# A fused two-block transformer kernel on one Trainium2 core: the first chunk behind a norm multiplied without the norm's root, in three feed-forwards of block one

## The chip, the cores and the metric

One of the eight cores of a Trainium2 chip runs the whole program. Times are device microseconds (us), the median of several runs. A core has five engines that work side by side and wait for each other by semaphores: TensorE (PE, matmuls), VectorE (DVE), ScalarE (ACT), GpSimd (POOL) and SyncE (SP), which here only issues the loads of weights.

## The reference

Two blocks of two layers each on x of 256 tokens by 1024. Only block one's feed-forwards are touched. Each of its layers has two, `f1` ahead of the mixers and `f2` behind them:

```python
D_MODEL, SEQ, D_FF = 1024, 256, 2816
def _rms_norm(x, g):
    xf = x.astype(jnp.float32)
    y = xf * lax.rsqrt(jnp.mean(xf * xf, axis=-1, keepdims=True) + EPS)
    return (y * g.astype(jnp.float32)).astype(x.dtype)
def _modulate(xn, shift, scale):
    return xn * (1 + scale[:, None, :]) + shift[:, None, :]
def _swiglu(x, w_in, w_out):
    gate, up = jnp.split(x @ w_in, 2, axis=-1)
    return (jax.nn.silu(gate) * up) @ w_out
...
mod = cond @ ada_w[l] + ada_b[l]
sh1, sc1, g1, sh2, sc2, g2, sh3, sc3, g3 = jnp.split(mod, N_MOD, axis=-1)
hn = _modulate(_rms_norm(h, norm_g[l, 0]), sh1, sc1)
h = h + 0.5 * g1[:, None, :] * _swiglu(hn, ffn1_w_in[l], ffn1_w_out[l])
...
hn = _modulate(_rms_norm(h, norm_g[l, 2]), sh3, sc3)
h = h + 0.5 * g3[:, None, :] * _swiglu(hn, ffn2_w_in[l], ffn2_w_out[l])
```

In words: each token (a column in the kernel) is divided by its root mean square, scaled and shifted per feature, and multiplied by `w_in`. A token's root is a factor of its whole column, so it commutes with the product; the shift does not carry it.

## The kernel before

**Layout.** Activations `h` lie as 8 k-tiles of 128 features by 256 tokens. A product takes weights in chunks of 1024 by 256 (8 k-tiles, 1 MB). SP loads them one after the other into a ring of four slots.

**Three terms.** For precision every operand is split in two fp32r parts. ScalarE rounds half a chunk at a time to `w_hi` (`round_half`, L1264), GpSimd subtracts to get `w_lo` (L700), and the activations have `hn` (high) and `hn_lo`. `terms` (L734) does hi x hi, hi x lo and lo x hi: six matmuls of 256 columns for a k-tile of a chunk (two column halves c, three terms), 48 for a chunk. `w_hi` and `w_lo` have two slots.

**Feed-forward** (`ffn`). `w_in` has 22 chunks in 11 pairs p: chunk 2p is the gate, 2p + 1 the value. Chunk 2p goes to PSUM bank 0 or 2, chunk 2p + 1 to bank 1 or 3, both column halves in one bank. ScalarE takes the SiLU (L1352), VectorE multiplies (L1836), and the product is split in two parts `gated` (L1359 on ScalarE, L1839 on VectorE). Bank reuse makes chunk 2p + 4 wait for pair p. In `f1` of pairs 1 to 8 and in layer 0's `f2` of pairs 1 to 6, VectorE also sums an `ada` chunk of 2 MB (L1701 to L1719), which will be modulation values later; SP loads it in the same sequence, into two buffers at the start of the arena. Then come 16 chunks of `w_out` in four groups g; after each, VectorE adds two tiles of the residual to `h` (marks `h f1 0` to `h f1 7` and so on).

**A norm.** ScalarE squares each new tile (L1292), VectorE adds the squares of tiles 0 to 5 up, and TensorE (`norm_sum`, L860 and L863) multiplies that sum and the squares of tiles 6 and 7 with a matrix of ones. ScalarE forms the root as exp(-0.5 ln x) (L1298, L1300). Then the chain runs through `h` by tiles: VectorE multiplies by gain and root into one of two PSUM tiles `normed` (L1796), ScalarE adds the shift and rounds to `hn` (L1324), VectorE forms `hn_lo` (L1805). Chunk 0 of the product follows with a loop of its own (L765, L766, L769), which takes each k-tile as it comes:

```python
for k in range(n if first else 0):
    kx, kw = k_tiles(phase, i)[0] + k0 + k, half * 4 + k
    pe.wait_ge(scalar_done, eng.at(f"hi {first} {kx}"))
    for c in range(2):
        ws = cols(c)[0]
        mm(outs[c], w_hi[:, q, kw, ws], hn[:, kx], start=kx == 0 and c == 0, stop=False)
        mm(outs[c], w_lo[:, q, kw, ws], hn[:, kx], start=False, stop=False)
    pe.wait_ge(vector_done, eng.at(f"split {first} {kx}"))
```

Six chunk 0s in the program wait for a root in this way: `f1`, `z` (the mixers' input) and `f2` of both layers. In `f1` of layer 0 the root is there early, since x comes from outside. In block two the first chunk is multiplied without the root already: `weigh` (L1310, L1311) makes tiles that carry the gain alone, and the root is applied to results.

**Order.** Each engine's program is written out by hand, one function per engine, and runs in that order; a wait holds up everything behind it on its engine.

## Time and profile before

| | |
|---|---|
| median of 3 runs | 1916.34 us (1914.74 to 1918.4) |
| the profiled execution | 1915.01 us |
| its span, first to last instruction | 1913.2 us |
| mean granted TensorE clock | 0.989 |
| TensorE, busy | 1856.1 us, 97% |
| weight loads of TensorE, busy | 1799.4 us, 94% |
| GpSimd, ScalarE, VectorE, busy | 1437.8, 988.2 and 916.9 us |
| matmuls at L734 on the chain that ended last | 78% of the span |
| mean DMA rate | 208 GB/s |

The median and the span don't measure the same: the runs include what lies around the first and the last instruction. In a timeline each line is an instruction, or several equal ones merged (x2), with its start, its length, and in brackets how long the engine had been idle before it and who released it. Matmuls overlap: a 256-column one is shown with 0.28 us but follows its neighbour in 0.11 us at full clock, so starts are to be compared, not lengths. The granted clock is a share of 2.4 GHz.

### The profile page before, as it was taken

How to read it: one execution, taken by the hardware profiler on the slowest of the kernel's cores; microseconds unless marked ns; L12 is line 12 of the kernel's file. 1: busy time of each engine (PE TensorE's matmuls, PEld its weight loads, DVE VectorE, ACT ScalarE, POOL GpSimd, SP SyncE). 2: the span in 40 equal slices, each digit the busy share in tenths (PEclk: the TensorE clock that was granted, in tenths of full speed). 3: DMA queues.
4: the chain of work that ended last, by engine and by line, in shares of the span. 5: the costliest groups of instructions: out<-in, count | busy, mean ns of one | idle time of the engine just before them, and what ended most of it. 6: DMA issues, size and time to landing. Idle time of an engine off the chain costs nothing.

```text
span 1913.2 us, 37040 instructions
## 1 busy us (share of the span) xinstructions
PE 1856.1 (97%) x15544; PEld 1799.4 (94%) x15544; DVE 916.9 (48%) x1817; ACT 988.2 (52%) x1531; POOL 1437.8 (75%) x660
## 2 busy tenths in 40 slices
PE   6999998999999999889999999999999999999999
PEld 3999997899999998879999998999999998999999
DVE  3676497485148676854132634253311634343321
ACT  2544466544454455655545345576554345575543
POOL 1888772688878887548888965588897965587896
PEclk8999999999999999999999999999999999999999
DMA  9999762695589896436556643455665643355662
GB/s 318 344 359 333 235 192 72 219 362 192 183 296 367 298 312 191 135 123 227 195 169 198 213 144 121 133 180 178 195 208 163 214 145 124 129 188 174 192 208 88
DMA packets 357109, 397.94 MB, mean 208 GB/s; under 512 B 9048, under 2 KB 319056, under 8 KB 356944
## 3 DMA queue, kind: packets, MB, share of 16 engines
q1 hardware_dynamic: 356032, 395.04, 63.0%
q8 instruction: 122, 2.00, 0.4%
q10 hardware_dynamic: 912, 0.55, 0.1%
q14 instruction: 43, 0.35, 0.1%
HBM read 394.51 MB, written 1.05 MB: 207 GB/s over the span
## 4 chain that ended last, share of the span: by engine, by line
PE 88%; SPq 3%; DVE 3%; ACT 2%; DMA 1%; POOL 1%; issue 1%; ACTq 0%; DVEq 0%
PE bank L734 78%; PE bank L1011 1%; PE bank L969 1%; POOL w_lo L700 1%; PE bank L765 1%; PE bank L769 1%; PE bank L766 1%; SPq L594 1%; ACT arena L1402 1%; PE bank L725 1%; SPq L604 1%; DVE arena L1926 1%; SPq L536 1%; DMA ring<-in_ffn_w_in 1%; SPq L575 1%
## 5 line engine op out<-in xcount | busy, mean ns | idle before, releaser
L700 POOL TENSOR_TENSOR w_lo<-ring,w_hi 128x1024 fp32r<-128x1024 f32 (+2 forms) x656 | 1437.5, 2219 | 460.6 <-ACT w_hi L1264 459.6
L1264 ACT ACTIVATE w_hi<-ring 128x1024 fp32r<-128x1024 f32 (+2 forms) x656 | 629.1, 983 | 394.5 <-PE bank L734 382.8
L734 PE MATMUL bank<-hn,w_hi 128*128 128x256 f32 x2752 | 770.6, 280 | 8.5 <-ACT arena L1581 4.9
L734 PE MATMUL bank<-hn_lo,w_hi 128*128 128x256 f32 x2752 | 763.2, 277 | 0.0
L734 PE MATMUL bank<-hn,w_lo 128*128 128x256 f32 x2752 | 763.2, 277 | 0.0
L734 PEld LDWEIGHTS bank<-hn,w_hi 128*128 128x128 f32 x2752 | 517.9, 188 | 13.7 <-ACT arena L1581 6.5
L734 PEld LDWEIGHTS bank<-hn,w_lo 128*128 128x128 f32 x2752 | 518.1, 188 | 0.0
L734 PEld LDWEIGHTS bank<-hn_lo,w_hi 128*128 128x128 f32 x2752 | 516.7, 188 | 0.9 <-issue 0.5
L734 PE MATMUL bank<-gated,w_hi 128*128 128x256 f32 x1408 | 241.9, 277 | 0.0
L734 PEld LDWEIGHTS bank<-gated,w_hi 128*128 128x128 f32 x1408 | 212.8, 188 | 0.0
L734 PE MATMUL bank<-gated,w_lo 128*128 128x256 f32 x704 | 195.2, 277 | 0.0
L734 PE MATMUL bank<-up,w_hi 128*128 128x256 f32 x1024 | 174.2, 276 | 0.0
L1704 DVE SCALAR_TENSOR_TENSOR bank<-arena,cond,bank 128x512 f32<-128x512 f32 x204 | 154.2, 756 | 7.3
L734 PEld LDWEIGHTS bank<-up,w_hi 128*128 128x128 f32 x1024 | 154.0, 188 | 0.0
L734 PE MATMUL bank<-up,w_lo 128*128 128x256 f32 x512 | 141.3, 276 | 0.0
L734 PEld LDWEIGHTS bank<-gated,w_lo 128*128 128x128 f32 x704 | 132.1, 188 | 0.0
L1352 ACT ACTIVATE arena<-bank 128x512 f32<-128x512 f32 x44 | 26.3, 598 | 155.4 <-PE bank L734 155.0
L1836 DVE TENSOR_TENSOR bank<-arena,bank 128x512 f32<-128x512 f32 x44 | 30.6, 696 | 155.7 <-PE bank L734 155.7
L1402 ACT ACTIVATE arena<-arena,stat 128x128 f32<-128x128 f32 x120 | 53.2, 444 | 91.1 <-DVE stat L1893 43.9
L734 PEld LDWEIGHTS bank<-up,w_lo 128*128 128x128 f32 x512 | 96.1, 188 | 0.0
L734 PE MATMUL bank<-w_hi,hn 128*128 128x256 f32 x288 | 84.0, 292 | 0.0
L734 PE MATMUL bank<-w_hi,hn_lo 128*128 128x256 f32 x288 | 80.3, 279 | 0.0
(237 smaller groups left out, 2440.2 us busy)
## 6 DMA issues: line engine op xcount, KB each, us to landing
ring<-in_ffn_w_in SPq DMA_DIRECT2D x88, 1024.0 KB, 7.3
ring<-in_w_in SPq DMA_DIRECT2D x72, 1024.0 KB, 5.2
arena<-in_ada_w SPq DMA_DIRECT2D x35, 2048.0 KB, 10.9
ring<-in_w_up SPq DMA_DIRECT2D x32, 1024.0 KB, 5.5
ring<-in_w_down SPq DMA_DIRECT2D x32, 1024.0 KB, 5.1
ring<-in_ffn_w_out SPq DMA_DIRECT2D x32, 768.0 KB, 5.4
ring<-in_ffn_w_out SPq DMA_DIRECT2D x32, 640.0 KB, 4.1
ring<-in_w_in SPq DMA_DIRECT2D x16, 512.0 KB, 3.7
```

The costliest lines, as they stand in the source:

```text
L536: queue.dma_start(dst, src).then_inc(rows_in, 16)
L575: sp.dma_start(ada[:, c % 2], ada_source(layer, c)).then_inc(ada_in[c % 2], 16)
L594: sp.dma_start(ring[:, s, k:k + n, :], src).then_inc(weights_in[s], 16)
L604: sp.dma_start(dst, src).then_inc(params_in, 16)
L700: pool.tensor_tensor(w_lo[:, q, ks], ring[:, r, k0:k0 + n], w_hi[:, q, ks], ALU.subtract) \
L725: i = pe.transpose(dst, src, ident[0:n, 0:n])
L734: last = mm(out, a, b, start=start and i == 0, stop=stop and i == 2)
L1264: f(w_hi[:, q, half * 4:half * 4 + n], ring[:, r, k0:k0 + n], ACT.Copy).then_inc(weights_rounded, 1)
L1352: f(act_tmp[:, j], bank[:, 2 * j], ACT.Silu).then_inc(silu_done, eng.step(f"{s} silu {p}", silu_done))
L1402: f(t, t, ACT.Exp, bias=st[:, b + j:b + j + 1], scale=scale, accum_out=st[:, 10 + 2 * m + j:11 + 2 * m + j]) \
L1704: stt(part, src[:, k], col(cond, k), part, ALU.mult, ALU.add).then_inc(vector_done, eng.step())
L1836: tt(bank[:, 2 * j], act_tmp[:, j], bank[:, 2 * j + 1], ALU.mult) \
```

## The change

It concerns `f2` of layer 0, `f1` and `f2` of layer 1. Layer 0's `f1` (`whole`) and both `z` keep the old way.

- While the products ahead of the norm run, ScalarE scales each new tile of `h` by the gain alone, twice (`weigh_parts`): to `normed` in PSUM and, rounded, to a new tile set `weighted_hi`; VectorE subtracts to `hn_lo` (`weighed_parts`). Squares, sum and root stay.
- `weighted_hi` has 258 columns that are used: column 256 holds the shift and 257 its rounding rest (`shift_columns`). The product so yields the 256 token columns and two that sum to the shift's contribution.
- TensorE (`weighted_product`) multiplies chunk 0 with these tiles, its column halves in banks 0 and 7, and does the norm's sum between k-tiles 1 and 2.
- ScalarE makes the root, copies it for all tokens (`token rstd`) and then runs the old chain for `hn`, which chunk 1 now takes tile by tile. In between it rounds chunk 1's second half and both halves of chunk 2, where the old chain had only chunk 1's second half.
- VectorE (`apply_root`) sums the two shift columns and multiplies both halves by the root into bank 0. The SiLU of pair 0 is done in halves with the shift as bias, behind the rounding of chunk 3.
- `hn_lo` is shared: VectorE waits for chunk 0's halves before it overwrites tiles 0 and 4. `weighted_hi` lies where an `ada` buffer lies: SP waits for chunk 0's end ahead of one `ada` load per place.

The diff's core (line numbers of hunks are the file's):

```diff
@@ -466,6 +466,8 @@
...
+        weighted_hi = {n: rounded(f"weighted_{n}", start, KT, S + 8) for n, start in (("f1", 4096), ("f2", 7168))}
@@ -571,6 +573,8 @@
...
                     sp.wait_ge(ada_summed, n - 1)
+                if (layer, c) in ((1, ADA_FIRST + 1), (0, 17), (1, 17)):
+                    sp.wait_ge(weights_used, eng.at("used f2in 0" if c == 17 else "used f1in 0"))
@@ -741,6 +745,28 @@
...
+            def weighted_product(phase, n, outs):
+                pe.wait_ge(vector_done, eng.at(f"h {n} {4 if n == 'f2' else 6}"))
+                for half in range(2):
+                    half_ready(phase, 0, half)
+                    for k in range(4):
+                        kx = 4 * half + k
+                        if kx == 2:
+                            norm_sum(n)
+                        pe.wait_ge(scalar_done, eng.at(f"weighted hi {n} {kx}"))
+                        for c in range(2):
+                            ws = slice(c * P, (c + 1) * P)
+                            mm(outs[c], w_hi[:, 0, kx, ws], weighted_hi[n][:, kx, 0:S + 2], start=kx == 0, stop=False)
+                            mm(outs[c], w_lo[:, 0, kx, ws], weighted_hi[n][:, kx, 0:S + 2], start=False, stop=False)
+                        pe.wait_ge(vector_done, eng.at(f"weighted split {n} {kx}"))
+                        for c in range(2):
+                            last = mm(outs[c][:, 0:S], w_hi[:, 0, kx, c * P:(c + 1) * P], hn_lo[:, kx],
+                                      start=False, stop=kx == KT - 1)
+                    last.then_inc(weights_used, eng.step(f"used {phase} 0" if half else f"half used {phase} 0", weights_used))
@@ -929,11 +955,16 @@
...
+                whole = (s, layer) == ("f1", 0)
...
+                        if not whole and p == r == 0:
+                            weighted_product(s + "in", s, (bank[:, 0, 0:S + 2], bank[:, 7, 0:S + 2]))
+                            continue
...
-                        product(s + "in", (2 * p + r,), (b[:, 0], b[:, 1]), first=s if p == r == 0 else None,
+                        product(s + "in", (2 * p + r,), (b[:, 0], b[:, 1]),
+                                first=s if p == 0 and r == (0 if whole else 1) else None,
@@ -1310,6 +1338,19 @@
...
+            def weigh_parts(n, ks):
+                gains = der[:, 0:8] if n == "f1" else der[:, 16:24]
+                for k in ks:
+                    act.wait_ge(vector_done, eng.at(f"h {n} {k}"))
+                    if k >= 2:
+                        act.wait_ge(vector_done, eng.at(f"weighted split {n} {k - 2}"))
+                    gain = gains[:, k:k + 1]
+                    f(normed[:, k % 2], h[:, k], ACT.Identity, scale=gain).then_inc(scalar_done, eng.step())
+                    f(weighted_hi[n][:, k, 0:S], h[:, k], ACT.Identity, scale=gain) \
+                        .then_inc(scalar_done, eng.step(f"weighted hi {n} {k}"))
@@ -1329,6 +1370,32 @@
...
+            def weighted_and_norm(n, phase, shift):
+                take_squares(n, (6, 7))
+                weigh_parts(n, (6, 7))
+                norm_root(n)
+                f(rstd[:], rstd[:], ACT.Exp, scale=-0.5).then_inc(scalar_done, eng.step(f"token rstd {n}"))
+                for k in range(KT):
+                    act.wait_ge(vector_done, eng.at(f"normed k {n} {k}"))
+                    f(hn[:, k, :], normed[:, k % 2], ACT.Identity, bias=mod[:, shift + k:shift + k + 1]) \
+                        .then_inc(scalar_done, eng.step(f"hi {n} {k}"))
+                    if k == 1:
+                        round_half(phase, 1, 1)
+                    if k == 4:
+                        act.wait_ge(weights_in[slot_of(phase, 2)], eng.arrived(phase, 2))
+                        round_half(phase, 2, 0)
+                    if k == 6:
+                        round_half(phase, 2, 1)
@@ -1336,21 +1403,29 @@
...
-            def ffn(s, following):
+            def ffn(s, following, whole=False):
...
+                    if p == 0 and not whole:
+                        round_chunk(s + "in", 3)
+                        act.wait_ge(vector_done, eng.at(f"root applied {s}"))
+                        for c in range(2):
+                            f(act_tmp[:, 0, c * S:(c + 1) * S], bank[:, 0, c * S:(c + 1) * S], ACT.Silu,
+                              bias=small[:, 60 + c:61 + c]) \
+                                .then_inc(silu_done, eng.step(f"{s} silu 0" if c else None, silu_done))
+                    else:
+                        act.wait_ge(weights_used, eng.at(f"used {s}in {2 * p}"))
@@ -1544,14 +1622,16 @@
...
                 take_squares("f2", (0, 1))
+                weigh_parts("f2", (0, 1))
...
                 round_chunk("f2in", 0)
                 take_squares("f2", (4, 5))
+                weigh_parts("f2", (4, 5))
                 act.wait_ge(weights_in[slot_of("f2in", 1)], eng.arrived("f2in", 1))
                 round_half("f2in", 1, 0)
-                take_squares("f2", (6, 7))
-                norm("f2", "f2in", 48, late=((4, 1),))
+                weighted_and_norm("f2", "f2in", 48)
@@ -1799,6 +1879,8 @@
...
                         dve.wait_ge(scalar_done, eng.at(f"hi {n} {k - 1}"))
+                        if used and k in (1, 5):
+                            dve.wait_ge(weights_used, eng.at(f"{'half ' if k == 1 else ''}used {used} 0"))
@@ -1819,7 +1901,39 @@
...
+            def weighed_parts(n, g):
+                for k in (2 * g, 2 * g + 1):
+                    dve.wait_ge(scalar_done, eng.at(f"weighted hi {n} {k}"))
+                    tt(hn_lo[:, k, :], normed[:, k % 2], weighted_hi[n][:, k, 0:S], ALU.subtract) \
+                        .then_inc(vector_done, eng.step(f"weighted split {n} {k}"))
+            def shift_columns(n, at_):
+                shifts, wide = mod[:, at_:at_ + 8], weighted_hi[n]
+                dve.tensor_copy(wide[:, :, S], shifts).then_inc(vector_done, eng.step())
+                dve.wait_ge(vector_done, eng.at())
+                tt(wide[:, :, S + 1], shifts, wide[:, :, S], ALU.subtract).then_inc(vector_done, eng.step())
+            def apply_root(n, phase):
+                dve.wait_ge(weights_used, eng.at(f"used {phase} 0"))
+                dve.wait_ge(scalar_done, eng.at(f"token rstd {n}"))
+                for c, b in enumerate((0, 7)):
+                    dve.tensor_reduce(small[:, 60 + c:61 + c], bank[:, b, S:S + 2], AX.X, ALU.add) \
+                        .then_inc(vector_done, eng.step())
+                dve.wait_ge(vector_done, eng.at())
+                for c, b in enumerate((0, 7)):
+                    tt(bank[:, 0, c * S:(c + 1) * S], bank[:, b, 0:S], rstd[:], ALU.mult) \
+                        .then_inc(vector_done, eng.step(f"root applied {n}" if c else None))
             def ffn(s, gate_at, layer, following):
+                if (s, layer) != ("f1", 0):
+                    apply_root(s, s + "in")
@@ -2132,8 +2253,9 @@
...
-                dve.wait_ge(vector_done, eng.at())
-                scale_norm("f2", lambda k: col(der, 16 + k), 48)
+                    weighed_parts("f2", i)
+                dve.wait_ge(vector_done, eng.at())
+                scale_norm("f2", lambda k: col(der, 16 + k), 48, "f2in")
```

How the order moves on TensorE, at layer 0's `f2`: `mix_hi` is the operand of the last product before the norm, `weighted_f_56` is `weighted_hi`. Before:

```order
L734 MATMUL bank<-mix_hi,w_lo 128x256
L860 MATMUL bank<-square_sum,const 128x256
L863 MATMUL bank<-square,const 128x256 x2
L765 MATMUL bank<-hn,w_hi 128x256
L766 MATMUL bank<-hn,w_lo 128x256
```

and of the change:

```order
L738 MATMUL bank<-mix_hi,w_lo 128x256
L762 MATMUL bank<-weighted_f_56,w_hi 128x258
L763 MATMUL bank<-weighted_f_56,w_lo 128x258
L762 MATMUL bank<-weighted_f_56,w_hi 128x258
L763 MATMUL bank<-weighted_f_56,w_lo 128x258
L766 MATMUL bank<-hn_lo,w_hi 128x256 x2
L762 MATMUL bank<-weighted_f_56,w_hi 128x258
L763 MATMUL bank<-weighted_f_56,w_lo 128x258
L762 MATMUL bank<-weighted_f_56,w_hi 128x258
L763 MATMUL bank<-weighted_f_56,w_lo 128x258
L766 MATMUL bank<-hn_lo,w_hi 128x256 x2
L886 MATMUL bank<-square_sum,const 128x256
```

Two k-tiles of chunk 0 have moved ahead of the norm's sum, and the number of matmuls is the same.

ScalarE at the same place, from the last two squares on. Before:

```order
L1292 ACTIVATE square<-h 128x256 x2
L1298 ACTIVATE rstd<-bank,const 128x256
L1300 ACTIVATE bank<-rstd 128x256
L1324 ACTIVATE hn<-bank,mod 128x256 x5
L1264 ACTIVATE w_hi<-ring 128x1024
L1324 ACTIVATE hn<-bank,mod 128x256 x3
L1281 ACT_TABLE_LOAD
L1352 ACTIVATE arena<-bank 128x512
```

and of the change, from the last of the four scalings on:

```order
L1351 ACTIVATE weighted_f_56<-h,der 128x256
L1326 ACTIVATE rstd<-bank,const 128x256
L1328 ACTIVATE bank<-rstd 128x256
L1379 ACTIVATE rstd<-rstd 128x256
L1382 ACTIVATE hn<-bank,mod 128x256 x2
L1292 ACTIVATE w_hi<-ring 128x1024
L1382 ACTIVATE hn<-bank,mod 128x256 x3
L1292 ACTIVATE w_hi<-ring 128x1024
L1382 ACTIVATE hn<-bank,mod 128x256 x2
L1292 ACTIVATE w_hi<-ring 128x1024
L1382 ACTIVATE hn<-bank,mod 128x256
L1309 ACT_TABLE_LOAD
```

Four scalings stand between the squares and the root, and three roundings inside the chain instead of one; the first SiLU has gone behind two more roundings.

## Rows read from the trace of the kernel before

**Rows 1.** The page, engines: busy us, share of the span, instructions.
```profile
PE 1856.1 (97%) x15544; PEld 1799.4 (94%) x15544; DVE 916.9 (48%) x1817; ACT 988.2 (52%) x1531; POOL 1437.8 (75%) x660
```
**Rows 2.** Who TensorE waited for: us in total, times, longest us.
```profile
PE bank L765 <- ACT hn L1324: 12.6, 6, 2.2
```
**Rows 3.** Timeline of TensorE, layer 0's f2: start us, length us, instruction.
```profile
358.96 0.59 PE L860 MATMUL bank<-square_sum,const 128*128 128x256 f32 x2
359.39 0.59 PE L863 MATMUL bank<-square,const 128*128 128x256 f32 x2
...
370.43 0.28 PE L734 MATMUL bank<-hn,w_hi 128*128 128x256 f32 x1
```
**Rows 4.** Timeline of TensorE, layer 1's f1.
```profile
544.51 0.59 PE L860 MATMUL bank<-square_sum,const 128*128 128x256 f32 x2
...
555.04 0.28 PE L765 MATMUL bank<-hn,w_hi 128*128 128x256 f32 x1
...
555.72 0.28 PE L734 MATMUL bank<-hn,w_hi 128*128 128x256 f32 x1
```
**Rows 5.** Timeline of TensorE, layer 1's f2.
```profile
853.97 0.59 PE L860 MATMUL bank<-square_sum,const 128*128 128x256 f32 x2
...
865.45 0.28 PE L734 MATMUL bank<-hn,w_hi 128*128 128x256 f32 x1
```
**Rows 6.** Stretches: busy per engine, then PEclk (granted clock), DMA share, GB/s.
```profile
45.50:52.50 7.00, 6.98 (x48) 6.05 (x49) 6.22 (x14) 4.84 (x9) 2.38 (x1) 1.00 1.05 373
364.40:368.30 3.90, 3.90 (x21) 3.90 (x21) 3.73 (x9) 2.79 (x6) 0.99 (x1) 0.56 0.81 259
549.00:552.60 3.60, 3.60 (x20) 3.60 (x19) 3.49 (x8) 2.22 (x4) 0.00 (x0) 0.53 1.09 358
...
1039.60:1045.30 5.70, 5.70 (x49) 5.62 (x49) 1.77 (x5) 4.49 (x10) 3.64 (x4) 1.00 0.61 194
590.00:610.00 20.00, 20.00 (x178) 20.00 (x178) 15.85 (x23) 8.77 (x11) 18.44 (x8) 1.00 1.08 366
```
**Rows 7.** Timeline of VectorE, layer 1's f1.
```profile
544.03 0.48 DVE L1859 SCALAR_TENSOR_TENSOR h<-bank,der,h 128x256 f32<-128x256 f32 x1 [12.14 <-PE bank L734]
...
547.43 0.88 DVE L1796 SCALAR_TENSOR_TENSOR bank<-h,der,bank 128x256 f32<-128x256 f32 x2 [2.24 <-ACT bank L1300]
...
554.70 0.48 DVE L1805 SCALAR_TENSOR_TENSOR hn_lo<-bank,mod,hn 128x256 fp32r<-128x256 f32 x1 [0.15 <-ACT hn L1324]
561.43 0.69 DVE L1836 TENSOR_TENSOR bank<-arena,bank 128x512 f32<-128x512 f32 x1 [6.25 <-PE bank L734]
```
**Rows 8.** Timeline of TensorE, block two's first chunk behind a norm.
```profile
1039.59 0.38 PE L765 MATMUL bank<-hn,w_hi 128*128 128x256 f32 x1
```
**Rows 9.** Timeline of ScalarE, layer 1's f1.
```profile
545.23 0.42 ACT L1292 ACTIVATE square<-h 128x256 f32<-128x256 f32 x1 [0.27 <-DVE h L1859]
546.44 0.47 ACT L1298 ACTIVATE rstd<-bank,const 128x256 f32<-128x256 f32 x1 [0.79 <-PE bank L863]
...
550.42 0.47 ACT L1324 ACTIVATE hn<-bank,mod 128x256 fp32r<-128x256 f32 x1 [0.44 <-DVE bank L1796]
```
**Rows 10.** Timeline of ScalarE, block two's first scalings: the first and the fourth.
```profile
1039.57 0.48 ACT L1310 ACTIVATE bank<-h,norm 128x256 f32<-128x256 f32 x1 [0.51 <-DVE h L1859]
...
1040.79 0.49 ACT L1311 ACTIVATE hn<-h,norm 128x256 fp32r<-128x256 f32 x1
```
**Rows 11.** Timeline of VectorE, one pair of layer 1's f1.
```profile
574.43 0.75 DVE L1701 TENSOR_SCALAR bank<-arena,cond 128x512 f32<-128x512 f32 x1
...
583.19 0.70 DVE L1836 TENSOR_TENSOR bank<-arena,bank 128x512 f32<-128x512 f32 x1 [0.98 <-PE bank L734]
```
**Rows 12.** Timeline of SyncE's queue: loads of layer 1's f1 chunks 18 to 21.
```profile
627.69 15.97 SPq L594 DMA_DIRECT2D ring<-in_ffn_w_in  x4
```
**Rows 13.** The first of these loads alone, from issue to landing.
```profile
DMA to landing us min/median/max: 11.6/11.6/11.6
```
**Rows 14.** Timeline of ScalarE: the rounding of chunk 18.
```profile
643.46 2.00 ACT L1264 ACTIVATE w_hi<-ring 128x1024 fp32r<-128x1024 f32 x2
```

43 lines of the change are left out of this document (27 added, 16 removed).

## The prediction

> **What bounds the kernel now.** I read the page first. TensorE is busy 97% of the span [rows 1]; the kernel is a stream of matmuls and gets shorter only where that stream has holes or runs slowly. The second view is who TensorE waited for: the largest entry is the first chunk behind a norm, L765 waiting for normalized activations, 12.6 us in 6 waits, none over 2.2 us [rows 2]. Three of those six places are changed.
>
> The third view is the timeline of TensorE at the three places: layer 0's f2 [rows 3], layer 1's f1 [rows 4] and layer 1's f2 [rows 5]. Each begins with the norm's sum (L860, L863); a hole of 2.2 us and the 48 matmuls of chunk 0 follow, and L734 begins with chunk 1. From the sum's first matmul to chunk 1 that is 370.43 - 358.96 = 11.47 us, 555.72 - 544.51 = 11.21 us and 865.45 - 853.97 = 11.48 us. What the work needs is in the same rows. The three float32 matmuls of the sum are 0.43 us apart (358.96 to 359.39), together 1.28 us. A k-tile of a chunk is six matmuls in 0.68 us (555.04 to 555.72), a chunk 5.44 us. That makes 6.72 us, so the excess is 4.75, 4.49 and 4.76 us: **14.00 us** in all.
>
> The fourth view, stretches with their granted clock, says what the excess is. Behind each hole a stretch of 3.6 to 3.9 us has a mean of 0.53 to 0.56 (the third place repeats the first) [rows 6], so nearly all of it at 1.2 GHz. It holds 20 or 21 matmuls, which take 2.3 to 2.4 us at 0.113 us each at the full clock: 1.3 to 1.5 us lost. The hole is 2.2 us, and short waits in chunk 0 are the rest.
>
> **The change, part by part.** *Chunk 0 no longer needs the root.* TensorE runs it on activations that carry the gain alone; those of k-tiles 0 to 5 exist before the last product ends. It does two k-tiles (1.36 us), the sum (1.28 us), and six more k-tiles. In f2 it starts at once. In f1 its bank is read by the residual addition h 6, which ends at 544.03 + 0.48 = 544.51 us, just when the last product's stream ends [rows 7]; I charge 0.1 us. The nearest case of this form is block two's first norm, whose chunk 0 also runs ahead of the root: it starts at 1039.59 us with no hole ahead of it [rows 8], and its 5.7 us have a granted clock of 1.00 [rows 6].
>
> *Are k-tiles 6 and 7 ready?* TensorE wants tile 6 at 544.6 + 1.36 + 1.28 + 2.72 = 549.9 us. ScalarE squares h 7 until 545.23 + 0.42 = 545.65 us [rows 9], and four scalings (two per k-tile) take 1.71 us where they exist, 1039.57 to 1041.28 us [rows 10]: ready at 547.4 us. Cost nothing, with 2.5 us of cover. The sum wants square 7 at 545.97 us, 0.3 us after it is there.
>
> *The root comes later, and chunk 1 needs it.* This is the wait that takes the old one's place. The scalings hold ScalarE until 547.4 us; the sum ends at 544.6 + 1.36 + 1.28 and 0.15 of latency, also 547.4. The first normalizing product on VectorE starts 547.43 - 546.44 = 0.99 us after the logarithm [rows 7, 9]: at 548.45 us, 1.0 us later than now. From that product to the end of the last subtraction there are 7.75 us now (547.43 to 554.70 + 0.48), with one half chunk rounded in between on ScalarE. The change rounds three there. VectorE paces this chain and leaves ScalarE 0.44 us idle per k-tile [rows 9], so two more roundings of 1.05 us cost between nothing and 2.1 us. I take 0.55: nearly nothing for the early one, which idle pieces make good, and 0.4 for the one ahead of the last k-tile, which has none behind it. So 8.3 us, and with the last two matmuls (0.25) chunk 1 ends at 557.0 us. TensorE alone would be at 544.6 + 1.28 + 10.88 = 556.8. So **0.2 us** of wait is left. In f2 ScalarE and sum are ready 2.8 to 2.9 us behind the start as well, and I take the same.
>
> *Two columns more.* 32 of a chunk's 48 matmuls have 258 columns. At the rate of 256 columns that is under 0.001 us each, 0.1 us for all 96. No row has this shape; its price lies between nothing and the 0.43 us of a float32 matmul [rows 3], and I take the near end, since operands and type are those of L765.
>
> *Root applied, SiLU in halves.* VectorE gets two small reductions and two 128x256 products (some 1.3 us), ScalarE a SiLU in halves, behind the table load and both halves of chunk 3. That puts pair 0's multiplication at 561.2 us, where it is at 561.43 now [rows 7]. TensorE wants its result when chunk 4 reuses the bank, at 557.0 + 10.9 = 567.9 us. Hidden, with 4 us of cover.
>
> *VectorE afterwards.* TensorE is 4 us earlier and VectorE hardly, with an `ada` sum of 7.8 us per pair (574.43 to 582.21 us) [rows 11]. So its multiplications lag by 2 to 3 us. Each result is wanted two chunks after the next pair begins, 8 us of slack now, and VectorE has 0.98 us idle per pair [rows 11]: the lag is gone after three pairs. Cost nothing.
>
> *Weights.* In layer 1's f1 the DMA engines are full (share 1.08, 366 GB/s) [rows 6]. Chunk 18's load, issued at 627.69 us [rows 12], takes 11.6 us [rows 13], so it has landed at 639.3, and is rounded at 643.46 us [rows 14]. That slack of 4.2 us is what TensorE gains. But ring slots are freed earlier too (chunks 1 to 3 are split 2 to 4 us earlier), so some 2.5 us stay, and GpSimd's split has more behind them. SP's new waits, for the end of chunk 0, stand behind the load of chunk 5, which waits for chunk 1's split; they cost nothing, and nothing is queued behind them that was earlier.
>
> *Work ahead of the norm.* The other scalings and subtractions load ScalarE and VectorE during the products before. Block two's first norm has the same load and no hole [rows 8]. Nothing.
>
> **The sum.** 14.00 us of excess go; 0.1 + 3 x 0.2 + 0.1 us come back: **13.2 us**. The profiled execution took 1915.01 us for a span of 1913.2; it would take 1901.8. The median of the runs, 1916.34 us, is 1.3 above it, so I forecast **1903.1 us**. A measurement of this kernel tells about 0.2%, 3.8 us, from no change.
>
> **A rule against the trace.** Each stretch at the lower clock came behind a hole of no more than 2.2 us [rows 2, 6]. A chunk paced at 7.0 us for 48 matmuls by the same VectorE chain, layer 0's first, kept the clock at 1.00 [rows 6], as did block two's gapless norm: so the hole is the likely cause, and it goes. The Trainium skill (TensorE: Matmul & The Clock Gate, section Why this matters for your kernels) asks only that idle gaps between bursts of matmuls stay under about 3 us. By that page a 2.2 us hole would do no harm, the fall would have another cause, and the sum would lose its share of the clock, which is the first rival below; the trace so far speaks against it.
>
> **Rivals.** *The clock falls all the same.* If the transition itself and not the hole lowers it, three stretches stay, at 1.3 to 1.6 us each: up to 1903.1 + 4.8 = 1908 us. Chance 0.10.
>
> *Chunk 1 waits much longer.* If the added roundings delay the chain in full, it takes 7.75 + 2.1 = 9.85 us, 1.55 more than I took, at three places: 1907.8 us. For it: they stand ahead of activations that VectorE waits for. Against it: ScalarE's idle pieces. Late weights or a VectorE that never makes up its lag, another 1 to 3 us in layer 1's f1, come to the same region, 1905 to 1911. Chance 0.09.
>
> *No gain.* Chunk 1 inherits the whole hole, or the new waits stop TensorE elsewhere: 1913 to 1919 us. Chance 0.03.
>
> *Slower.* If 258 columns are not multiplied at the fast rate, being more than the 256 of every other such matmul, each could cost the 0.43 us of a float32 matmul where it costs 0.113: 96 x 0.32 = 30 us, and 1933 us. This turns the result from 13.2 / 96 = 0.14 us more per matmul on. Against it: nothing in the timeline ties the rate to 256. Chance 0.05.
>
> The forecast has the rest, 0.73. The range runs from the whole excess gone, with 2 us of spread (1900), to the clock rival (1908.5). Faster by over 0.2%: 0.73 + 0.10 + 0.09 = 0.92; within: 0.03; slower: 0.05.
>
> **What would show it.** Right: the last product runs into chunk 0 with no hole, and the sum comes 1.4 us in; the granted clock is 1.00 at all three places; from the first matmul behind the last product to chunk 2 there are 12.3 to 12.5 us, where the same stretch has 16.7 to 16.9 now; 258-column matmuls stand 0.114 us apart; the waits of the entry in rows 2 shrink to three. Wrong: waits of over 0.5 us inside chunk 1, a low clock behind the sum, waits for weights or for the products of pairs 1 to 8, or a saving far from 4.4 us per place.

## The result, and the profile after

The changed kernel takes **1895.71 us** (6 runs, 1893.11 to 1898.37) beside 1915.54 us of the kernel before, a ratio of 0.9889 [0.9863, 0.9915]. It is faster, as forecast, but the time lies 4 us below the range: 19.8 us gained instead of 13.2. Run three more times beside the kernel before it took 1897.04, 1896.20 and 1896.19 us, with ratios of 0.9919 [0.9897, 0.9941], 0.9898 [0.9876, 0.9921] and 0.9902 [0.9864, 0.9939]. The kernel before has a median of 1914.79 us over the 95 runs that stood beside the experiments. So the gain is **18.6 us**, 5 more than forecast; in the four comparisons it was 19.8, 14.8, 18.6 and 19.8 us.

The page's engines, after (compare [rows 1]):
```profile
span 1891.3 us, 37169 instructions
PE 1839.2 (97%) x15544; PEld 1787.5 (95%) x15544; DVE 937.4 (50%) x1859; ACT 1008.0 (53%) x1585; POOL 1437.1 (76%) x660
```
The changed kernel's waits of TensorE (line; us in total, times, longest). The entry of [rows 2], 12.6 us in six waits, has shrunk to the three places that were not changed. The weights' entry, L738 for GpSimd's w_lo, holds 4.9 us where it held 3.6, but that is not the change's doing: a second profile of the kernel before has 4.7 us in eight waits, the longest 1.6 too, and the long ones lie in layer 0's first feed-forward:
```profile
PE bank L791 <- ACT hn L1365: 6.1, 3, 2.2
PE bank L738 <- POOL w_lo L704: 4.9, 8, 1.6
```
The changed kernel's timeline of TensorE at layer 1's f1 (start us, length us, instruction), for [rows 4]:
```profile
534.37 0.28 PE L738 MATMUL bank<-gated,w_lo 128*128 128x256 f32 x1
534.54 0.39 PE L762 MATMUL bank<-weighted_f,w_hi 128*128 128x258 f32 x1
534.76 0.28 PE L763 MATMUL bank<-weighted_f,w_lo 128*128 128x258 f32 x1
534.88 0.28 PE L762 MATMUL bank<-weighted_f,w_hi 128*128 128x258 f32 x1
...
536.09 0.59 PE L886 MATMUL bank<-square_sum,const 128*128 128x256 f32 x2
536.52 1.03 PE L889 MATMUL bank<-square,const 128*128 128x256 f32 x4
537.19 0.47 PE L762 MATMUL bank<-weighted_f,w_hi 128*128 128x258 f32 x1
...
541.69 0.28 PE L791 MATMUL bank<-hn,w_hi 128*128 128x256 f32 x1
...
547.13 0.28 PE L738 MATMUL bank<-hn,w_hi 128*128 128x256 f32 x1
```
The last product runs into chunk 0 (L762) with no hole, the sum (L886, L889) comes 1.55 us in, chunk 1 (L791) takes 547.13 - 541.69 = 5.44 us, which is its work and no wait. Counted over 102 matmuls, from the start of the first one behind the last product to the start of chunk 2, a place measures 12.49 us in layer 0's f2, 12.59 in layer 1's f1 and 12.49 in layer 1's f2; before it was 16.91, 16.65 and 16.92. That is 4.42 + 4.06 + 4.43 = **12.9 us**.

Stretches of the changed kernel (each engine's busy us and instructions, then the granted clock, DMA share, GB/s): the three places have 1.00, where [rows 6] have 0.53 to 0.56.
```profile
353.30:365.90 12.60, 12.60 (x105) 12.45 (x105) 9.07 (x23) 10.81 (x21) 8.06 (x5) 1.00 0.89 309
534.50:547.10 12.60, 12.60 (x104) 12.41 (x103) 8.99 (x22) 10.85 (x21) 9.22 (x5) 1.00 0.92 318
838.40:851.00 12.60, 12.60 (x105) 12.44 (x104) 9.10 (x23) 10.59 (x21) 7.40 (x4) 1.00 0.83 289
```
The spans of the two profiled executions differ by 1913.2 - 1891.3 = 21.9 us, so 9.0 us are elsewhere: 2.9 up to the end of layer 0's first feed-forward, 2.7 and 1.5 in the two layers' mixers, where before has a stretch of 6.8 us at half the clock that the changed kernel's profile lacks, and 1.8 in block two. None lies in the streams behind the three places. The first piece is in code that the change does not touch. The same 20 us of layer 0's first feed-forward, TensorE alone, in the kernel before and in the changed one:
```profile
62.00:82.00 20.00, 20.00 (x172) 1.00 1.05 347
```
```profile
62.00:82.00 20.00, 20.00 (x179) 1.00 1.05 342
```
TensorE is busy for all of either, at a granted clock of 1.00, and yet starts 172 matmuls in one and 179 in the other. An unbroken stream of these 256-column matmuls goes at one of **two paces**, one every 0.1133 us or one every 0.1178 us, and keeps it for as long as nothing interrupts it. A feed-forward has some 1,530 behind its first chunks: 1,530 x 0.0045 = 6.9 us between a fast and a slow stream. My sum took each unchanged stream to cost the same before and after.

### The profile page after: what moved, and what is told of

Its sections match the earlier page's. It is cut to its first block, busy times and chain, and to the rows that moved or that the text cites. A ratio compares the mean times of both kernels' runs of the same rounds, so it can differ in the third digit from the quotient of the medians.

```text
span 1891.3 us, 37169 instructions
## 1 busy us (share of the span) xinstructions
PE 1839.2 (97%) x15544; PEld 1787.5 (95%) x15544; DVE 937.4 (50%) x1859; ACT 1008.0 (53%) x1585; POOL 1437.1 (76%) x660
## 4 chain that ended last, share of the span: by engine, by line
PE 88%; DVE 3%; SPq 3%; ACT 2%; DMA 1%; POOL 1%; issue 1%; ACTq 0%; DVEq 0%
PE bank L738 78%; PE bank L1042 1%; PE bank L1000 1%; POOL w_lo L704 1%; SPq L598 1%; PE bank L791 1%; PE bank L792 1%; PE bank L795 1%; ACT arena L1479 1%; SPq L608 1%; SPq L538 1%; DMA ring<-in_ffn_w_in 1%; PE bank L729 1%; DVE arena L2044 1%; DMA arena<-in_ada_w 1%
## 5 line engine op out<-in xcount | busy, mean ns | idle before, releaser
L738 PE MATMUL bank<-hn,w_hi 128*128 128x256 f32 x2704 | 755.8, 280 | 9.8 <-ACT arena L1661 4.9
L738 PE MATMUL bank<-hn,w_lo 128*128 128x256 f32 x2704 | 748.4, 277 | 0.0
L738 PE MATMUL bank<-hn_lo,w_hi 128*128 128x256 f32 x2704 | 748.4, 277 | 0.0
L738 PEld LDWEIGHTS bank<-hn,w_hi 128*128 128x128 f32 x2704 | 508.5, 188 | 15.1 <-ACT arena L1661 6.5
L738 PEld LDWEIGHTS bank<-hn_lo,w_hi 128*128 128x128 f32 x2704 | 508.1, 188 | 0.9 <-issue 0.5
L738 PEld LDWEIGHTS bank<-hn,w_lo 128*128 128x128 f32 x2704 | 507.9, 188 | 0.0
L738 PE MATMUL bank<-gated,w_hi 128*128 128x256 f32 x1408 | 239.6, 276 | 0.0
L738 PEld LDWEIGHTS bank<-gated,w_hi 128*128 128x128 f32 x1408 | 211.7, 188 | 0.0
L738 PE MATMUL bank<-gated,w_lo 128*128 128x256 f32 x704 | 194.3, 276 | 0.0
L738 PE MATMUL bank<-up,w_hi 128*128 128x256 f32 x1024 | 174.2, 276 | 0.0
L738 PEld LDWEIGHTS bank<-up,w_hi 128*128 128x128 f32 x1024 | 154.2, 188 | 0.0
L738 PE MATMUL bank<-up,w_lo 128*128 128x256 f32 x512 | 141.3, 276 | 0.0
L738 PEld LDWEIGHTS bank<-gated,w_lo 128*128 128x128 f32 x704 | 132.2, 188 | 0.0
L738 PEld LDWEIGHTS bank<-up,w_lo 128*128 128x128 f32 x512 | 96.1, 188 | 0.0
L738 PE MATMUL bank<-w_hi,hn 128*128 128x256 f32 x288 | 84.0, 292 | 0.0
L738 PE MATMUL bank<-w_hi,hn_lo 128*128 128x256 f32 x288 | 80.2, 279 | 0.0
```

Source lines behind the costliest of these rows:

```text
L738: last = mm(out, a, b, start=start and i == 0, stop=stop and i == 2)
```

## The experiments

The surplus is what the gain has beyond the places, 18.6 - 12.9 = 5.7 us. Its theories fall in two groups. **A, C:** which stream is slow is chance in either kernel. **B, S, D:** the old form makes the streams behind the three places slow more often (B in any way, S by the hole, D by the clock's rise behind it). Diffs are against the kernel that the text names.

**The two kernels again.** No edit.

> The kernel before once more, unchanged. The profiled execution of before shows a second effect beside the holes: the matmuls of one unbroken stream follow each other either in 0.113 us or in 0.118 us, and layer 0's first feed-forward (57 to 232 us, 1487 matmuls) ran at 0.118 although the changed kernel ran the same code at 0.113. Theory A (chance): the pace of a stream is drawn anew in each execution, and the surplus of the changed kernel over my sum (19.8 us measured against 13.2) is such draws and two stretches of low clock in the attention. Then this profile has another set of slow streams than the first one, and single times spread over 8 to 12 us. Theory B (fixed): the pace belongs to the kernel; then this profile has the same slow streams again, layer 0's first feed-forward among them, and low clock again in both attentions. Ratio 1.000 within 0.002 under both.

> The changed kernel once more. Theory A (chance): a gain of 13 to 16 us against the kernel before, less than the first 19.8, and in the profile other streams at 0.118 us per matmul than in its first profile. Theory B (the gain elsewhere is systematic): 18 to 21 us again, the profile again with layer 0's first feed-forward at 0.113 and no low clock in the attentions. Both: from the first matmul behind the last product to chunk 2 some 12.4 to 12.9 us at each of the three places, where before has 16.7 to 16.9.

Measured: 1912.14 us for the kernel before (ratio 1.0001 [0.9982, 1.0019]) and 1897.04 for the changed one, the second of the four comparisons above. In before's new profile the fast and the slow stream have changed places. Behind layer 0's f2, layer 1's f1 and layer 1's f2:
```profile
400.00:420.00 20.00, 20.00 (x179) 20.00 (x178) 15.84 (x23) 8.88 (x11) 18.31 (x8) 1.00 1.07 367
600.00:620.00 20.00, 20.00 (x172) 20.00 (x171) 15.02 (x22) 7.98 (x11) 17.17 (x8) 1.00 1.07 369
900.00:920.00 20.00, 20.00 (x178) 20.00 (x178) 2.78 (x4) 9.09 (x11) 18.09 (x8) 1.00 0.61 200
```
So the pace of these streams is not fixed to the code. At the third place the clock did not fall in this execution; the place still took 16.59 us (two more such, in before_reset below, 16.59 and 16.57), beside 16.65 to 16.99 with a fall. **In the old form the low clock itself costs 0.4 us at most:** chunk 0 waits for the norm's chain anyway.

**One place, or two.** The change kept in one set of places, undone elsewhere:
```diff
+WEIGHTED = (('f1', 1),)                  # only_f1
+WEIGHTED = (('f2', 0), ('f2', 1))        # only_f2
-                whole = (s, layer) == ("f1", 0)
+                whole = (s, layer) not in WEIGHTED
```


> The change at layer 1's first feed-forward alone; both second feed-forwards as before. My sum: 4.2 us of gain, 1911 us where before has 1915.5. Theory A: 4.2 us, give or take the draws, which 5 rounds leave at 1.5 us. Theory B with the surplus spread over the places: 6 to 7 us.

> The change at the two second feed-forwards alone; layer 1's first as before. My sum: 2 x 4.5 = 9.0 us of gain. Theory A: 9 us, give or take 1.5. Theory B: 13 us. If the places add up, this gain and that of the first feed-forward alone make the gain of the whole change.

Measured: 1907.94 us (0.9973 [0.9957, 0.9990]) and 1904.83 us (0.9960 [0.9942, 0.9978]), 5.2 and 7.6 us gained by the ratios, give or take 3.2 and 3.4. Places measure 12.49 to 12.60 us in the new form and 16.8 to 17.0 in the old, in one kernel side by side; they alone would give 4.1 and 8.9. Only_f1 leaves both theories open. Only_f2 speaks against theory B, which put 13 us, and lies nearer to A's 9. Beside the changed kernel on the same chip (1897.04) the same two are 10.9 and 7.8 us slower, where the places left in the old form are worth 8.9 and 4.1: seen from there 2 to 4 us more are lost. At this size the times do not decide, and the traces have to. The stretches of only_f1 behind an old, the new, and an old place:
```profile
400.00:420.00 20.00, 20.00 (x172) 20.00 (x172) 15.95 (x22) 8.66 (x10) 16.38 (x8) 1.00 1.07 363
600.00:620.00 20.00, 20.00 (x179) 20.00 (x178) 15.88 (x22) 10.20 (x12) 17.25 (x8) 1.00 1.07 366
900.00:920.00 20.00, 20.00 (x173) 20.00 (x172) 2.78 (x4) 9.31 (x11) 17.45 (x8) 1.00 0.59 187
```
Both streams behind an old place are slow, the one behind the new place is fast. Over the profiles so far, three of nine streams behind an old place were slow and none of nine behind a new one: a hint for theory B, against the time of only_f2.

**A hole put back.** Changed kernel:
```diff
                             norm_sum(n)
+                            pe.wait_ge(vector_done, eng.at(f"normed k {n} 1"))
```


> Computes the same. The changed kernel, but TensorE is made to wait behind each of the three norm sums until VectorE has made the normed k-tile 1, a hole of some 2.2 us as before, with nothing else undone. Forecast's mechanism: the hole costs its 2.2 us less the some 0.3 us of chunk 1's waits for the chain that it swallows, and the clock falls behind it (about 1.4 us more), so a place measures 15.5 to 16.2 us from its first matmul to chunk 2 instead of 12.5, and the kernel takes 9 to 12 us more than the changed kernel. Rival (the low clock comes of something else, the two feeds of block one's chain say): the clock stays at 1.0, a place measures 14.2 to 14.6, the kernel 5 to 7 us more. Theory of the surplus S (the pace of 0.113 or 0.118 us a matmul is drawn where a stream is entered, and behind a hole a third of the streams of 1,480 matmuls draws the slow one): of the three streams behind the places about one is slow here in the profile, and the timed runs stand another 3 to 7 us higher and scatter more. Theory C (which pace a stream takes has nothing to do with the hole): the three streams are all at 0.113 and the sum above holds without more.

Measured: 1912.69 us (0.9996 [0.9971, 1.0021]), 1903.67 to 1929.51. The clock fell at one place of three. TensorE's timeline there, and stretches of TensorE alone behind the three holes:
```profile
848.13 0.42 PE L763 MATMUL bank<-weighted_f,w_hi 128*128 128x258 f32 x1 [2.00 <-DVE bank L1877]
848.35 0.42 PE L764 MATMUL bank<-weighted_f,w_lo 128*128 128x258 f32 x1
```
```profile
359.00:362.40 3.40, 3.40 (x30) 1.00 0.74 233
542.50:545.90 3.40, 3.40 (x30) 1.00 1.01 333
848.00:851.40 3.40, 3.27 (x16) 0.55 0.92 297
```
The places measure 14.76, 14.83 and, with the fall, 16.28 us: a hole of 2.0 us idle costs 2.25 us, and the low clock 1.5 us where TensorE is not held up by anything else. All three streams behind were fast in the profile, whose execution was the quickest of the twelve. The median lies 16.5 us above the changed kernel's, where three holes and three falls explain 3 x (2.25 + 1.5) = 11.3 us, and the runs scatter over 26 us. For S, but not proof.

**Sizes and order in the place.** Changed kernel; cols256 leaves out the shift:
```diff
-mm(outs[c], w_hi[:, 0, kx, ws], weighted_hi[n][:, kx, 0:S + 2], start=kx == 0, stop=False)
+mm(outs[c], w_hi[:, 0, kx, ws], weighted_hi[n][:, kx, 0:S], start=kx == 0, stop=False)   # cols256
-                    if k == 4:
+                    if k == 7:                                                           # late_rounds
                         act.wait_ge(weights_in[slot_of(phase, 2)], eng.arrived(phase, 2))
                         round_half(phase, 2, 0)
-                    if k == 6:
                         round_half(phase, 2, 1)
```


> Leaves out the shift's part of chunk 0 at the three places (the weighted matmuls run over 256 columns, and VectorE adds two other columns in place of the shift's). Forecast's price of the 258 columns (nothing a matmul, 32 of them at each of three places): places of 12.4 to 12.5 us as in the changed kernel and the same time within 0.2%. Rival (each matmul of 258 columns, or the odd length, costs more): 32 x 3 of them at up to 0.1 us, a place shorter by 0.3 us or more and the kernel 1 to 9 us faster than the changed kernel.

> Computes the same. ScalarE's two roundings of chunk 2 stand behind the chain instead of behind k-tiles 4 and 6. If the chain with the roundings in it holds chunk 1 up, chunk 1's waits go: a place of 12.0 to 12.3 us instead of 12.5, and the kernel up to 1 us faster. If chunk 2 then comes late (its two halves must also be subtracted on GpSimd, some 2.2 us each), a wait of 1 to 3 us stands ahead of chunk 2 and the kernel is 2 to 8 us slower. Forecast: the chain holds it by 0.2 us, the roundings come late by about as much; the same within 0.3%.

cols256: 1898.55 us (0.9915 [0.9887, 0.9942]), places of 12.42, 12.52 and 12.42: two more columns cost 0.07 us a place. late_rounds: 1908.92 us (0.9968 [0.9947, 0.9990]), places of 14.5 to 14.6: I missed this one. The roundings in the chain cost nothing, and behind it chunk 2 is 2.0 us late. Three such waits are 6 us of the 12.7 that this version takes more than the changed kernel. Its timelines of TensorE at layer 0's f2 and at layer 1's f2 show more:
```profile
365.92 0.39 PE L795 MATMUL bank<-hn_lo,w_hi 128*128 128x256 f32 x2
368.15 0.39 PE L738 MATMUL bank<-hn,w_hi 128*128 128x256 f32 x1 [1.85 <-POOL w_lo L704]
368.37 0.28 PE L738 MATMUL bank<-hn_lo,w_hi 128*128 128x256 f32 x1
```
```profile
857.99 0.38 PE L738 MATMUL bank<-hn,w_hi 128*128 128x256 f32 x1 [1.85 <-POOL w_lo L704]
...
859.04 0.41 PE L738 MATMUL bank<-hn,w_hi 128*128 128x256 f32 x1
...
861.82 0.33 PE L738 MATMUL bank<-hn_lo,w_hi 128*128 128x256 f32 x1
861.98 0.28 PE L738 MATMUL bank<-hn,w_lo 128*128 128x256 f32 x1
```
and the stretches behind the three places:
```profile
400.00:420.00 20.00, 20.00 (x179) 20.00 (x178) 15.84 (x23) 9.14 (x11) 17.24 (x8) 1.00 1.07 368
600.00:620.00 20.00, 20.00 (x179) 20.00 (x178) 15.87 (x22) 10.20 (x12) 17.23 (x8) 1.00 1.07 365
900.00:920.00 20.00, 20.00 (x172) 20.00 (x171) 2.77 (x4) 9.60 (x11) 17.14 (x8) 1.00 0.57 183
```
The same wait of 1.85 us stands at all three. Behind the third alone the clock fell (0.41 us a matmul), rose again inside the running stream at 861.8 us, and that stream alone is slow. In all these profiles, the slow streams behind a place are four of the ten at which the clock had fallen, and none where it had not. That is theory D: **the clock's rise draws the pace.** It holds for these streams; other interruptions move the pace as well, as the next part shows.

**What sets the pace.** Changed kernel, extra work ahead of chunks of the feed-forwards' first product:
```diff
+if phase == "f1in" and half == 0 and not first:                             # kicks: layer 0, layer 1
+    mm(outs[0][:, 0:1], ones[0:1, 0:P], ones[0:1, 0:1], start=True, stop=True)
+    mm(outs[0][:, 0:P], ones, ones, start=True, stop=True)
+if (phase, kick_layer) in (("f2in", 0), ("f1in", 1)) and half == 0 and not first and i % 2:   # kicks256
+    for t in range(3 if kick_layer else 1):
+        mm(outs[0], ones, square_sum[:], start=True, stop=True)
+if phase in ("f1in", "f2in") and half == 0 and not first and i % 3 == 2:   # breaks
+    for _ in range(100 if kick_layer else 12):
+        pe.sem_inc(pad, 1)
```


> Computes the same. Ahead of every chunk but the first of block one's first feed-forward TensorE makes one extra 32-bit matmul into the chunk's own bank, overwritten at once: in layer 0 of 1 row and 1 column (as the root's columns in block two are made), in layer 1 of 128 rows and 128 columns. Theory K (the form of what interrupts a stream sets the pace behind it): all stretches behind the small one run at one pace (0.118, as behind the root's columns), all behind the large one at the other (0.113). Theory R (each interruption draws anew, at random): both layers show stretches of either pace, about a third at 0.118. Theory L (only a wait, not another kind of matmul, can change it): each layer keeps one pace through all its stretches. The extra matmuls themselves cost some 0.1 to 0.5 us each, so the kernel may be 3 to 12 us slower.

> Computes the same. Ahead of every second chunk of the first product, in layer 0's second feed-forward one extra 32-bit matmul of 128 rows and 256 columns, in layer 1's first feed-forward three of them (as a norm's sum), all overwritten at once. In the profile with extra matmuls of 1 and of 128 columns the pace turned over at every one of them, 0.113 and 0.118 us in turn. Theory T (every such interruption turns the pace over): 0.113 and 0.118 in turn behind single ones and behind triple ones. Theory W (a norm's sum sets the pace to 0.113 whatever it was, as all eight stretches behind the norm's sums of block two in the profiles so far say): all stretches behind the triples at 0.113. The extra matmuls cost 0.3 us each: 11 + 33 of them, about 13 us.

> Computes the same. Ahead of every third chunk of the first products of block one's four feed-forwards (7 places in each) TensorE's own queue counts up an unused semaphore, 12 times in layer 0 (a short pause, under 1 us) and 100 times in layer 1 (a pause of several us), with nothing else changed: 14 short and 14 long pauses in streams of 256-column matmuls. Theory D (the clock's rise in the middle of a stream draws the pace): behind every long pause the clock falls, comes back some 3 to 7 us later inside the stream, and the pace behind it is 0.118 us in about a third of the 14 cases (3 to 7) and 0.113 in the others; behind the 14 short ones the clock stays and the pace follows a fixed rule (all the same, or turned over each time, as behind the extra matmuls). Rival P (any pause draws it): a mix behind the short ones too. Rival O (the pace has nothing to do with the clock): the long ones leave the pace as the short ones do. The kernel becomes slower by the pauses, some 50 to 120 us, which says nothing else.

kicks took 1914.03 us (0.9995 [0.9976, 1.0013]), kicks256 1917.65, breaks 2134.03 (one run each). None of K, R and L held in kicks: behind both forms the pace **turns over** each time, 0.113, 0.118, 0.113 and so on, 21 and 20 times in a row. kicks256, behind four single matmuls, and then behind two of the triples:
```profile
364.00:374.00 10.00, 10.00 (x91) 10.00 (x90) 6.15 (x16) 8.61 (x13) 9.42 (x5) 1.00 0.86 294
376.00:386.00 10.00, 10.00 (x87) 10.00 (x86) 8.98 (x14) 4.51 (x5) 9.10 (x5) 1.00 1.02 331
387.50:397.50 10.00, 10.00 (x90) 10.00 (x89) 8.02 (x12) 4.64 (x6) 8.84 (x4) 1.00 1.08 365
399.00:409.00 10.00, 10.00 (x88) 10.00 (x87) 7.29 (x11) 4.48 (x5) 8.99 (x4) 1.00 1.08 364
...
577.00:586.00 9.00, 9.00 (x82) 9.00 (x81) 5.79 (x9) 3.50 (x4) 8.98 (x4) 1.00 1.08 364
589.00:598.00 9.00, 9.00 (x82) 9.00 (x81) 5.72 (x9) 3.69 (x5) 8.79 (x4) 1.00 1.07 368
```
One turns it over, ten times of ten; three in a row, the form of a norm's sum, leave it fast, ten times of ten (theory W). In breaks eight of the short pauses left a gap. The seven that set two matmuls 0.5 to 0.7 us apart turned the pace over, one of 1.5 us did not. Layer 0's first four:
```profile
62.00:92.00 30.00, 30.00 (x258) 30.00 (x257) 23.92 (x34) 13.03 (x16) 24.03 (x11) 1.00 1.04 348
96.00:126.00 30.00, 30.00 (x267) 30.00 (x267) 24.98 (x35) 13.76 (x16) 25.14 (x11) 1.00 1.07 361
130.00:160.00 30.00, 30.00 (x257) 30.00 (x256) 17.62 (x24) 13.50 (x16) 24.12 (x11) 1.00 1.06 368
164.00:194.00 30.00, 30.00 (x267) 30.00 (x267) 25.18 (x35) 13.95 (x19) 24.70 (x15) 1.00 0.91 308
```
That is no rule of pauses in general. Waits for weights in layer 0's first feed-forward interrupt the stream by themselves: 29 of 0.5 to 2.5 us, from start to start, in 18 profiles (all but kicks and breaks). Behind 16 of them the pace had changed, in either direction, behind 13 not; of the six of 0.5 to 0.7 us one changed it. In only_f2 a wait at 123.6 us (0.70 from start to start) leaves the stream fast, one at 135.5 us (1.06) turns it slow; TensorE alone, ahead of, between and behind them:
```profile
108.00:123.00 15.00, 15.00 (x135) 1.00 1.07 367
124.50:134.50 10.00, 10.00 (x91) 1.00 1.06 336
136.50:146.50 10.00, 10.00 (x87) 1.00 1.08 374
```
And behind the first four long pauses of breaks (13.5 to 15 us, at half the clock until 3 to 6 us into the stream):
```profile
580.00:590.00 10.00, 10.00 (x91) 10.00 (x90) 3.50 (x5) 5.10 (x6) 8.27 (x4) 1.00 0.22 70
611.00:621.00 10.00, 10.00 (x87) 10.00 (x86) 7.90 (x11) 4.57 (x6) 5.92 (x3) 1.00 0.32 107
645.00:655.00 10.00, 10.00 (x87) 10.00 (x87) 3.24 (x5) 5.10 (x6) 8.23 (x4) 1.00 0.22 67
676.00:686.00 10.00, 10.00 (x87) 10.00 (x86) 7.81 (x11) 4.48 (x6) 5.90 (x3) 1.00 0.36 107
```
Behind a rise of the clock I found no rule: the fourteen give fast, slow, slow, slow, fast, fast, fast, slow, fast, fast, slow, fast, fast, slow. Six of 14, with the four of ten above **10 of 24**.

**The pace set in both kernels.** The same triple set behind the clock's rise in both kernels:
```diff
+if half == 0 and (phase, i, kick_layer) in (("f2in", 2, 0), ("f1in", 2, 1), ("f2in", 2, 1)):
+    for t in range(3):
+        mm(outs[0], ones, const[:, at["ident"]:at["ident"] + S], start=True, stop=True)
```


> Computes the same. The kernel before, with three extra 32-bit matmuls of 128 rows and 256 columns (which set the pace behind them to 0.113 us in the last profile, ten times of ten) ahead of chunk 2 in each of the three feed-forwards that the change touches, behind the clock's rise. Theory D (behind the clock's rise the stream of the feed-forward draws the slow pace in some 4 of 10 cases, which costs it about 1,530 x 0.0045 = 6.9 us, and the new form takes this away): all three streams at 0.113; the extra matmuls cost some 0.8 us a place, the draws no longer cost 0.4 x 6.9 = 2.8 us a place, so it is 4 to 8 us faster than before and scatters less. Theory C (the surplus was chance, and the streams' pace costs before no more than after): 2 to 3 us slower than before.

> Computes the same. The changed kernel with the same extra matmuls at the same three chunks. Both theories: its streams are at 0.113 already, so it gains nothing and is 2 to 3 us slower than the changed kernel. Against before_reset, in which the pace is set as well, theory D says that what is left is the places themselves: 4.0 to 4.3 us each, 12 to 13 us in all. Theory C says that what is left is the whole difference of the two kernels, 15 to 19 us.

Measured: before_reset 1914.11 us (0.9993 [0.9976, 1.0010]), after_reset 1902.47 (0.9937 [0.9912, 0.9962]). **They differ by 11.6 us**, where the kernels without the triples differ by 18.6 and the places alone by 12.9. The triples cost the changed kernel some 6 us, more than I had put (its traces show 1.1 us each and 0.2 us in the stream behind, so 3.9 us; the rest is unexplained). In the kernel before they cost nothing on balance, and the scatter shrank from a standard deviation of 4.8 us (17 runs) to 2.3 (12 runs). That they gave back there in fast streams what they took is a reading of mine that its profile does not show: in that execution the clock fell at one place of three, and the matmuls ahead of all three triples ran at 0.113 already. Taken by itself before_reset missed the 4 to 8 us of theory D; the difference is what it forecast. By the ratios' intervals it is 11 us give or take 6, so it decides nothing alone, and theory D leans on the traces.

**What the rule buys elsewhere.** Behind the two small matmuls of block two's root_columns, 389 matmuls ran slow in each profile.
```diff
                     if p == 4:
                         root_columns(layer)
+                        mm(bank[:, 7, S:S + P], ones, ones, start=True, stop=True)      # toggle2
+                        for t in range(3):                                             # fast_entries
+                            mm(bank[:, 7, S:2 * S], ones, const[:, at["ident"]:at["ident"] + S], start=True, stop=True)
+if half == 0 and (phase, i) == ("z2", 6):                                              # kick_ahead
+    mm(outs[0][:, 0:1], ones[0:1, 0:P], ones[0:1, 0:1], start=True, stop=True)
```


> Computes the same. The changed kernel with one extra 32-bit matmul of 128 columns into an unused stretch of a bank behind the two small ones for the root's columns in either layer of block two. Theory T: it turns the 389 matmuls behind it from 0.118 us to 0.113 in both layers, worth 389 x 0.0045 = 1.75 us each, less some 0.3 us for the matmul: 2.9 us faster than the changed kernel. Rival (those streams are at 0.118 for their operands, not for how they are entered): they stay at 0.118 and the kernel is 0.6 us slower.

> The changed kernel once more, for the comparison on this chip and for three more entries of streams. Theory D (in the new form no clock rises in the stream behind a place, so none of the three is at 0.118): all three at 0.113. Theory C (the pace of those streams is chance in either form, a third at 0.118): one of three on average at 0.118. The time 14 to 17 us below before.

> Computes the same. The changed kernel with the same three extra matmuls behind the root's columns in either layer of block two, where the 389 matmuls behind ran at 0.118 us in every profile, and ahead of chunk 4 of layer 0's first feed-forward, behind the clock's rise there. Theory W: all three stretches run at 0.113. Behind the root's columns 1.75 us less some 0.8 for the matmuls, twice; in layer 0 6.5 us in some 4 of 10 executions less 0.8: 3 to 4 us faster than the changed kernel in all, and a narrower scatter. Rival (the stretch behind the root's columns is slow for its operands): no gain there, 0 to 1 us faster in all.

> Computes the same. The version with the pace set at three stretches once more, beside the changed kernel on the same chip. By the traces the three extra matmuls cost 1.0 to 1.2 us where they stand, against 1.75 us behind the root's columns (twice) and 6 us in some 4 of 10 executions in layer 0: 2 to 3 us faster than the changed kernel by theory, 0 if a stretch elsewhere turns over.

> Computes the same. The changed kernel with one extra 32-bit matmul of 1 row and 1 column ahead of the last chunk before the root's columns in either layer of block two. Theory T2 (the two small matmuls of the root's columns turn the pace over once, whatever it was): the 48 matmuls of that chunk run at 0.118, the 389 behind the root's columns at 0.113: 1.75 us less, 0.4 us more in each layer, 2 to 3 us faster than the changed kernel in all. Rival (the root's columns, behind which TensorE has waited, set the slow pace whatever it was, as a norm's sum sets the fast one): the 389 stay at 0.118 and the kernel is 0.5 to 1 us slower.

> The changed kernel once more, on the same chip as the two versions. 14 to 19 us below before; its three streams behind the places all at 0.113 by theory D, one of them at 0.118 on average by theory C.

toggle2: 1897.18 us (0.9909 [0.9889, 0.9929]); the 389 stay slow, so theory T fails where matmuls of two forms follow on one another. fast_entries, with a triple in layer 0's f1 as well: 1894.49 (0.9897 [0.9873, 0.9922]) and again 1895.85 (0.9894 [0.9858, 0.9930]); all three stretches are fast behind the triples in both profiles, but in layer 0's f1 only as far as a wait for weights at 148 and at 135 us, and slow from there on (172 or 173 matmuls in 20 us). kick_ahead: 1895.47 (0.9893 [0.9853, 0.9934]). Behind the root's columns, kick_ahead and the changed kernel's fourth profile:
```profile
1054.00:1099.00 45.00, 45.00 (x395) 44.91 (x394) 18.88 (x41) 17.94 (x23) 36.87 (x16) 1.00 0.58 187
```
```profile
1051.00:1096.00 45.00, 45.00 (x383) 45.00 (x383) 18.49 (x38) 16.74 (x20) 36.07 (x16) 1.00 0.57 185
```
One matmul ahead of the root's columns turns the stretch behind them fast, as T2 says: 1.0 us less from the first matmul of that part to 640 later, in both layers. The time of either version lies within 1 us of the changed kernel's on the same chip (1896.19), less than these runs can tell; no version was found that clearly beats it. In the four profiles of the changed kernel all twelve streams behind a place are fast, and so are the 15 of cols256, toggle2, both fast_entries and kick_ahead.

## Why the prediction was wrong in size

*What bounds the kernel, and where the gain is:* right. The waits shrank to three, the hole and the low clock are gone at all three places.

*The place* was right as a whole: 12.3 to 12.5 us forecast, 12.49, 12.59 and 12.49 measured. Inside it small terms were off and met. Chunk 1 does not wait (0.2 us put, none measured; the roundings in the chain cost nothing). Chunk 0 runs at 0.12 us a matmul, with 256 columns in cols256 too, and takes 5.9 to 6.0 us where I had 5.44; the sum takes 1.11 where I had 1.28. Together that is 0.3 to 0.4 us more than the needs I took. Against 4.4 us a place the three give 4.42, 4.06 and 4.43: 12.9 us where I had 13.2.

*The excess* I had split into hole, low clock (1.3 to 1.5 us) and short waits as if they added up. They don't: with no fall the old place was shorter by 0.4 us at most, since the matmuls then wait for the chain. The 1.5 us is right only where nothing else holds TensorE up (the hole experiment). The sum is untouched by this, since it took the excess as a whole, and the price of the first rival, 1.3 to 1.6 us a place in the new form, fits.

*The step that failed is the sum itself:* "14.00 us of excess go", and all else costs what it did. It priced the clock's fall by the matmuls that ran in it, and the streams behind the places at nothing. By the traces the larger part of the fall's price comes later: in 10 of 24 cases the clock's return leaves the stream behind at 0.118 us a matmul, for 6.9 us. At nine of the twelve old places in the profiles the clock had fallen: 3 x 9/12 x 0.42 x 6.9 = 6.5 us on average, an estimate from those counts. 12.9 + 6.5 = 19.4 beside 18.6 measured, and the pair with the triples leaves 18.6 - 11.6 = 7.0 for it, give or take 6. What is shown is that four of the ten streams behind a fall were slow and none of those without one; that this is the whole of the 5.7 us is not shown. Against it stands the time of only_f2. One more stretch is slow in both profiles of the kernel before and in none of the other eighteen: the last 420 matmuls ahead of the last norm's sum of block two, for 1.9 us; no experiment followed it. That there are two paces was to be seen in the profile before: 172 matmuls in one stretch of 20 us, 179 in others.

*The profiled execution* of before drew all three streams behind the places fast and layer 0's slow, so the extra 9.0 us in the first comparison of traces are not theory D's and count as chance, while the surplus of the medians is not. These two must be kept apart.

*A rule against the trace.* The clock fell behind gaps of 2.0 to 2.2 us, at nine of twelve old places and once in three with the hole put back; behind gaps of 1.85 us once in three. The Trainium skill (TensorE: Matmul & The Clock Gate, section Why this matters for your kernels) asks for idle gaps under about 3 us. By that the places would have been harmless; the traces disagree, and as forecast the fall went with the hole. One witness of mine fails: layer 0's first chunk, paced by the chain behind a gap of 1.7 us, kept the clock at 1.00 [rows 6] in that one profile only. In the other nineteen the clock is low over part of it. The same stretch in the changed kernel's first profile:
```profile
45.50:52.50 7.00, 6.82 (x37) 6.85 (x38) 6.32 (x14) 4.83 (x10) 2.40 (x1) 0.60 1.05 374
```

*258 columns, the root's application, VectorE's lag, weights:* hidden or nearly nothing, as put (the two columns cost 0.2 us in all, 0.1 put).

Open is why a stream has two paces at all, when a wait moves it from one to the other, what share of the surplus lies outside the three streams, and why the triples cost after_reset 6 us in time and 3.9 in the trace.

## What to carry to other kernels

Before you sum up a change, count the matmuls per 20 us in streams with no wait and a full granted clock, in both kernels: a difference of 4% there is a cost that no wait table shows. A hole ahead of a long stream can be worth more than its own length, for if the clock falls in it, its return can leave the whole stream at the slow pace. Where two causes hold the same instructions up (a low clock and a chain), price the removal of one with the other still in place.
